# Partners of rotated queries and keys by DMA copies instead of matmuls, the minima ahead of a low half, a take ahead of the sigmoids

## What is computed

```
def _partial_rotary(x, pos):                      # on q (16 heads of 64) and on k (4 heads of 64)
    half = ROT_DIM // 2                           # ROT_DIM = 16
    x1 = x[..., :half];  x2 = x[..., half:ROT_DIM]
    rot = jnp.concatenate([x1 * cos - x2 * sin, x2 * cos + x1 * sin], axis=-1)
    return jnp.concatenate([rot, x[..., ROT_DIM:]], axis=-1)

def _hybrid_layer(h, ...):
    proj = h @ w_in
    (c_val, c_glu, c_gate, q, k, v, a_gate, r_x, r_gate) = jnp.split(proj, split_pts, axis=-1)
    c = c_val * sigmoid(c_glu);  c = silu(layer_norm(causal_depthwise_conv(c)))
    y_conv = (c @ conv_pw_w + conv_pw_b) * silu(c_gate)
    q = _partial_rotary(q, pos);  k = _partial_rotary(k, pos)
    y_attn = sliding_window_sink_attention(q, k, v, sinks) * silu(a_gate)
    y_lru = rg_lru(causal_depthwise_conv(r_x)) * silu(r_gate)       # two sigmoid gates inside
    mixed = jnp.concatenate([y_conv, y_attn, y_lru], axis=-1) @ w_out
    return _layer_norm(ALPHA * h + mixed, ...)
```

## Time and profile before

| | |
|---|---|
| median of 3 runs | 2737.76 us (2734.89 to 2743.21) |
| profiled execution | 2740.33 us, span 2738.5 us, mean granted PE clock 0.997 |
| PE | 2713.5 us busy, 99% |
| DVE, ACT, POOL | 1826.0, 1406.7, 142.8 us busy |
| DMA | 173 GB/s mean |
| second block | about 1941 us to the end; layer 0's projection from 1943, layer 1's from 2345 |

### The profile page before, as it was taken

One profiled execution on the slowest core, in us unless ns is written; L12 is line 12 of the kernel. 1 busy time (PEld: TensorE's weight loads), 2 busy tenths in 40 slices (PEclk: granted clock), 3 DMA queues, 4 the chain that ended last, 5 costly groups with the idle time before them and its releaser, 6 DMA issues.

```text
span 2738.5 us, 45092 instructions
## 1 busy us (share of the span) xinstructions
PE 2713.5 (99%) x16965; PEld 2422.5 (88%) x16965; DVE 1826.0 (67%) x2398; ACT 1406.7 (51%) x2142; POOL 142.8 (5%) x138
## 2 busy tenths in 40 slices
PE   8999999999999999999999999999999999999998
PEld 7888888888888888888888888888999899999897
DVE  7566565655665575665666656755888885789786
ACT  6444444444454454444444444544565774556764
POOL 0000000000000001010010101000000000000000
PEclk9999999999999999999999999999999999999999
DMA  7556655555655556655555655556554445554463
GB/s 232 180 177 184 180 178 178 180 180 177 184 173 187 185 158 181 182 178 180 179 178 179 184 179 179 176 184 187 171 168 128 127 154 172 167 155 146 132 202 129
DMA packets 472600, 474.43 MB, mean 173 GB/s; under 512 B 17674, under 2 KB 467746, under 8 KB 472226
## 3 DMA queue, kind: packets, MB, share of 16 engines
q1 hardware_dynamic: 472244, 472.87, 56.1%
q10 hardware_dynamic: 256, 0.18, 0.0%
HBM read 470.86 MB, written 2.13 MB: 173 GB/s over the span
## 4 chain that ended last, share of the span: by engine, by line
PE 93%; DVE 4%; ACT 2%; issue 1%; DMA 0%; SPq 0%; ACTq 0%; DVEq 0%
PE proj L1280 34%; PE proj L1282 17%; PE proj L1295 9%; PE proj L1467 6%; PE proj L1468 6%; PE proj L1469 6%; PE proj L1297 4%; PE proj L1722 2%; PE ps_s L1371 1%; PE ps_s L1354 1%; PE proj L1724 1%; DVE w_both L2146 1%; PE ps_t L1361 1%; PE ps_s L1372 1%; PE ps_s L1353 1%
## 5 line engine op out<-in xcount | busy, mean ns | idle before, releaser
L1280 PE MATMUL proj<-operand,w_both 128*128 128x512 f32 x4096 | 1453.4, 399 | 2.2 <-DVE w_both L1821 2.1
L1821 DVE TENSOR_TENSOR w_both<-w_raw,w_both 128x1024 fp32r<-128x1024 f32 x644 | 805.6, 1253 | 694.5 <-ACT w_both L673 693.2
L673 ACT ACTIVATE w_both<-w_raw 128x1024 fp32r<-128x1024 f32 x644 | 681.8, 1059 | 920.4 <-PE proj L1282 707.7
L1282 PE MATMUL proj<-operand,w_both 128*128 128x256 f32 x4096 | 1145.9, 280 | 0.0
L1280 PEld LDWEIGHTS proj<-operand,w_both 128*128 128x128 f32 x4096 | 769.0, 188 | 185.0 <-issue 2.4
L1282 PEld LDWEIGHTS proj<-operand,w_both 128*128 128x128 f32 x4096 | 772.9, 189 | 0.8
L1467 PE MATMUL proj<-operand,w_both 128*128 128x272 f32 (+2 forms) x1540 | 450.7, 293 | 0.1
L1468 PE MATMUL proj<-operand,w_both 128*128 128x272 f32 (+2 forms) x1540 | 442.5, 287 | 0.0
L1469 PE MATMUL proj<-operand,w_both 128*128 128x272 f32 (+2 forms) x1540 | 442.2, 287 | 0.0
L2146 DVE TENSOR_TENSOR w_both<-w_raw,w_both 128x1024 fp32r<-128x1024 f32 x226 | 277.5, 1236 | 133.5 <-ACT w_both L883 132.6
L1295 PE MATMUL proj<-w_both,operand 128*128 128x512 f32 x1024 | 363.2, 399 | 0.0
(11 more groups left out here) (383 smaller groups left out, 2055.1 us busy)
## 6 DMA issues: line engine op xcount, KB each, us to landing
w_raw<-in_a_w_in_dram SPq DMA_DIRECT2D x256, 512.0 KB, 3.7
w_raw<-in_w_in_dram SPq DMA_DIRECT2D x160, 512.0 KB, 3.6
w_raw<-in_b_w_in_dram SPq DMA_DIRECT2D x128, 512.0 KB, 3.9
w_raw<-in_kv_w_dram SPq DMA_DIRECT2D x128, 512.0 KB, 4.0
w_raw<-in_a_w_out_dram SPq DMA_DIRECT2D x64, 512.0 KB, 3.5
w_raw<-in_b_w_out_dram SPq DMA_DIRECT2D x64, 512.0 KB, 4.6
w_raw<-in_w_out_dram SPq DMA_DIRECT2D x64, 512.0 KB, 3.5
scratch<-in_a_rel_bias_dram SPq DMA_DIRECT2D x16, 256.0 KB, 3.6
```

The source lines that it names most:

```text
L673: act.activation(w_hi[:, s], w_raw[:, s], ACT.Copy).then_inc(hi_ready, 1)
L1280: pe.matmul(proj[:, 2 * bank + t, :], w_hi[:, s, kk, cols], rhs[:, k, :], start=first and k == 0, stop=False)
L1282: m = pe.matmul(proj[:, 2 * bank + t, 0:S], w_lo[:, s, kk, cols], rhs[:, k, 0:S], start=False, stop=last and end)
L1821: dve.tensor_tensor(w_lo[:, s], w_raw[:, s], w_hi[:, s].bitcast(F32), ALU.subtract).then_inc(pieces_split, 1)
```

## The change

- `perm` and `spread` go, with their two loads. `spread_keys` and `exchange_queries` go from PE: eight f32 matmuls for the keys and eight for the queries in each layer.
- ACT gets `fetch_partners(n, tile)`: four SBUF to SBUF copies of eight partitions each (the two rotated half-ranges of both heads, 2176 B a partition), issued on ACT's own queue: once for the keys behind `shift_kv(0)` and once for each query unit behind its take. The partners go to `rc`, which POOL sets to zero once a layer (`memset`, `pads_ready`); it is used as two buffers, so the third copy on waits for a rotation (`q_rotated`).
- The keys are now rotated once where they stand, by the same `rotate` as the queries (DVE, three instructions of 544 columns for all four heads), and then spread to both halves by four copies of 64 partitions (`spread_keys` on ACT), which `score` and ACT's first `set_sinks` wait for.
- `score(i)` waits for the rotation of its own queries only (`5 * l + i // 2 + 2`), and for all value copies.
- From the second pair on, `score_maxima(i)` stands ahead of the pair's first low half.
- At i = 6 the take of unit 16 stands ahead of the sigmoids instead of two high halves behind the first.

```diff
@@ gpsimd
+            pool.wait_ge(glu_fixed, 1)
+            pool.memset(rc, 0.0).then_inc(pads_ready, 1)
             for l in range(DEPTH):
...
+                if l + 1 < DEPTH:
+                    pool.wait_ge(gate_used, 5 * l + 5)
+                    pool.memset(rc, 0.0).then_inc(pads_ready, 1)
@@ scalar
+                def fetch_partners(n, tile):
+                    half = ROT // 2
+                    for first in (0, HD):
+                        for to, of in ((first, first + half), (first + half, first)):
+                            act.dma_start(partners[n % 2][to:to + half], tile[of:of + half]).then_inc(partners_landed[n % 2], 16)
+
+                def spread_keys():
+                    act.wait_ge(q_rotated, 5 * l + 1)
+                    for h in range(2):
+                        for e in range(2):
+                            act.dma_start(k_spread[HD * h:HD * h + HD, e::2, :], k_raw[HD * e:HD * e + HD])\
+                               .then_inc(k_spread_landed, 16)
+
                 shift_kv(0, k_raw)
+                act.wait_ge(kv_ready, 2 * l + 1)
+                act.wait_ge(pads_ready, l + 2)
+                fetch_partners(0, k_raw)
                 hi(1)
                 affine(3)
                 take_raw(5)
...
-                take(U_Q, att[:, 0:2, :], cols=live)
+                def take_queries(j):
+                    take(U_Q + j, att[:, 2 * j:2 * j + 2, :], cols=live)
+                    act.wait_ge(proj_free, o0 + U_Q + j + 3)
+                    if j == 1:
+                        act.wait_ge(q_rotated, 5 * l + 1)
+                    if j >= 2:
+                        act.wait_ge(q_rotated, 5 * l + j)
+                    fetch_partners(j + 1, att[:, 2 * j:2 * j + 2, :])
+
+                take_queries(0)
                 hi(1)
                 shift_kv(1, v_raw)
-                hi(3)
-                take(U_Q + 1, att[:, 2:4, :], cols=live)
+                hi(2)
+                spread_keys()
+                hi(1)
+                take_queries(1)
                 for j in range(2, 4):
                     hi(4)
-                    take(U_Q + j, att[:, 2 * j:2 * j + 2, :], cols=live)
+                    take_queries(j)
...
                     if i == 6:
                         take_recurrent(3)
                         hi(1)
+                        act.wait_ge(gate_used, 5 * l + 1)
+                        take(unit, a_gates[:, 4:6, :], 0.5, cols=live)
                         act.wait_ge(lru_taken, 4 * l + 4)
                         act.activation(lru_r, lru_r, ACT.Sigmoid)
                         act.activation(lru_i, lru_i, ACT.Sigmoid).then_inc(lru_gates, 1)
@@ tensor
                 for chunk in range(PIECES):
                     pe.wait_ge(in_split, 4 * l + chunk + 1)
                     pieces(U_Q, norm, (chunk,))
-                    if chunk == 1:
-                        spread_keys(0)
-                pieces(U_Q + 1, norm, (0, 1))
-                spread_keys(1)
-                pieces(U_Q + 1, norm, (2, 3))
+                pieces(U_Q + 1, norm, (0, 1, 2, 3))
...
-                pieces(U_Q + 2, norm, (2,))
-                exchange_queries(0, ps_s)
-                pieces(U_Q + 2, norm, (3,))
-                pieces(U_Q + 3, norm, (0,))
-                exchange_queries(1, ps_t)
-                pieces(U_Q + 3, norm, (1, 2))
-                exchange_queries(2, ps_s)
-                pieces(U_Q + 3, norm, (3,))
+                pieces(U_Q + 2, norm, (2, 3))
+                pieces(U_Q + 3, norm, (0, 1, 2, 3))
 
                 def score(i):
-                    pe.wait_ge(q_rotated, 4 * l + (3 if i == 0 else 4))
-                    pe.wait_ge(k_spread_ready, KV_HEADS * l + KV_HEADS)
+                    pe.wait_ge(q_rotated, 5 * l + i // 2 + 2)
+                    pe.wait_ge(k_spread_landed, 16 * 4 * (l + 1))
+                    pe.wait_ge(v_all_ready, 3 * l + 3)
@@ vector
+                def rotate(n, tile, scale, cols):
+                    part = partners[n % 2][:, :, cols]
+                    dve.wait_ge(partners_landed[n % 2], 16 * 4 * ((3, 2)[n % 2] * l + n // 2 + 1))
+                    dve.scalar_tensor_tensor(tile, tile, scale, over(cos[:, cols], 2), ALU.mult, ALU.mult)
+                    step(dve.scalar_tensor_tensor(part, part, scale, over(sin[:, cols], 2), ALU.mult, ALU.mult))
+                    dve.tensor_tensor(tile, tile, part, ALU.add).then_inc(q_rotated, 1)
...
-                rotate_keys(0)
                 lo(1)
                 dve.wait_ge(proj_free, o0 + U_V + 3)
                 fix(v_raw, U_V, kv_fixed)
                 lo(2)
-                rotate_keys(1)
+                rotate(0, k_raw, 1.0, slice(0, T))
...
                 for i in range(PAIRS_2):
-                    lo(1)
                     if i == 0:
-                        rotate_queries(3, ps_t)
+                        lo(1)
+                        rotate_queries(3)
                     score_maxima(i)
+                    if i >= 1:
+                        lo(1)
```

More of the change, by code:

```diff
@@ L118, in shape_constants @@
     cos, sin = np.ones((P, T), np.float32), np.zeros((P, T), np.float32)
-    partner = np.zeros(HD, int)
     for d in range(ROT):
-        partner[d] = d + half if d < half else d - half
         for e in range(2):
@@ L267, in build_program @@
         cos, sin = two.take(T), two.take(T)
-        perm = two.take(P)
-        spread = two.take(4, P)
         twice, head_of = two.take(4 * META), two.take(2)
@@ L421, in build_program @@
         conv_in = sem("conv_in")
-        kv_turned = sem("kv_turned")
-        k_spread_ready = sem("k_spread_ready")
+        partners_landed = [sem(f"partners_landed_{n}") for n in range(2)]
+        k_spread_landed = sem("k_spread_landed")
         v_turned = sem("v_turned")
@@ L565, in _ @@
                 sp.dma_start(sinks[:, l, :], io["attn_sinks_2"][l:l + 1, :].to_broadcast([P, HEADS_2])).then_inc(rows_landed, 16)
[L566 to L567 removed]
+            for dst, name in ((mask_2, "mask_2"), (cos, "cos"), (sin, "sin"), (twice, "twice"), (head_of, "head_of")):
                 at, n = const_at[name]
@@ L1532, in _ @@
                 if l == 0:
-                    pe.wait_ge(consts_2_in, 16 * 7)
-                def spread_keys(r):
-                    pe.wait_ge(kv_ready, 2 * l + 1)
-                    if r == 1:
-                        pe.wait_ge(k_spread_ready, KV_HEADS * l + 2)
-                    for e, banks in ((0, ps_s), (1, ps_t)):
-                        for turned_side in range(2):
-                            m = pe.matmul(banks[:, turned_side, 0:T], spread[:, 2 * e + turned_side, :], k_raw[:, r, :],
-                                          start=True, stop=True)
-                        m.then_inc(kv_turned, 1)
+                    pe.wait_ge(consts_2_in, 16 * 5)
                 def turn_values():
-                    pe.wait_ge(k_spread_ready, KV_HEADS * l + 4)
                     pe.wait_ge(kv_ready, 2 * l + 2)
@@ L1559, in double_meta_values @@
                       .then_inc(v_meta_doubled, 1)
-                def exchange_queries(r, banks):
-                    pe.wait_ge(proj_free, o0 + U_Q + r + 3)
-                    if r == 0:
-                        pe.wait_ge(v_all_ready, 3 * l + 3)
-                    if r >= 2:
-                        pe.wait_ge(q_rotated, 4 * l + r - 1)
-                    for e in range(2):
-                        m = pe.matmul(banks[:, e, live], perm, att[:, 2 * r + e, live], start=True, stop=True)
-                    m.then_inc(q_turned, 1)
                 for chunk in range(PIECES):
```

53 lines of the change are left out of this document (9 added, 44 removed).

## The result

The changed kernel takes 2748.82 us (median of 6 runs, 2746.28 to 2751.29) against 2737.38 us for the kernel before (6 runs, 2734.89 to 2743.21). The ratio is 1.004, 95% interval 1.003 to 1.005: slower by 0.4%, where I had forecast 2731.4, a gain of 6.4 us (0.23%; the prediction rounds it to 0.24), within 2722 to 2738. The measured time is outside the range and on the other side.

What follows compares the result with a forecast made beforehand. PE, busy 99% of the span, was taken as the bound. 23.0 saved - (1.8 + 2.0) - (2.6 + 1.4) - (2.0 + 3.4) - 3.4 = 6.4 us gained, from 2737.76 to 2731.4 us; range 2722 to 2738.

Steps and rivals of the forecast that it cites:

- Matmuls that go: Key and query matmuls removed from PE in both layers: 7.4 + 7.1, together 14.5 us saved.
- The take: Take moved ahead of the sigmoids: PE's stall at the conv sums goes, 5.2 us, plus clock, together 8.5 us.
- What is given back behind it: Conv branch behind the earlier take: later waits of PE return 2.0 us in layer 0, 3.4 in layer 1.
- The price of an issue: Each partner copy's issue on ACT was taken at 0.42 us, four at 1.7 us.
- 1.8 + 2.0: New PE stalls for the first query unit's fourth-piece operand, behind the keys' issues: 1.8 us layer 0, 2.0 layer 1.
- Most places hide it, since ACT waits for PE between its high halves there. One does not: ACT's copy issues cost nothing except at the keys' fetch, where some 1.2 of 1.7 us push the rest back.
- The first transposes: First pair of heads: DVE cannot follow PE, new PE stalls of 2.6 us in layer 0 and 1.4 in layer 1.
- Clock: PE's clock lowered after two of the new stalls, charged as two losses, 3.4 us.
- The issues starve PE: Rival, chance 0.06: keys' fetch between shift_kv and in_hi_of(3) delays PE; slower from 1.0 us an issue, 2750 at 2.56.

Runs made afterwards that it cites:

- the minima alone: Kernel before with only the mask minus scores and minima ahead of the first low half from the second pair on, no copies, take unmoved: 2733.95 us, ratio 0.9994.

## Why the prediction was wrong, step by step

**Matmuls that go: right.** 14.5 us forecast, 14.3 in the shifts.

**The take: right at its place,** 8.5 forecast and 8.4 measured, wait and clock together. What is given back behind it, forecast at 2.0 + 3.4, was 1.3 + 2.6: right in kind, 1.5 us too high. With the minima alone I costed nothing before the sigmoids, and the stretch to there did not change.

**The price of an issue: mis-sized.** I took 0.42 us, "since it is ACT's own". The row was of the right engine and the wrong kind: both of its issues read DRAM. The copies cost 0.63, and 1.25 the first. This turned 1.8 + 2.0 into 3.2 + 3.1 at the operand. At the DRAM price the same formula came out within 0.3 us. I had even asked what the price hangs on, and looked at the size (rightly: it hardly matters) and not at the source. The Trainium skill (DMA: Bandwidth & Descriptors, Anatomy of one DMA) puts the sequencer's dispatch at about 50 ns. Its breakdown is of a DMA issued from GpSimd and lists the making of descriptors beside the dispatch, so I was wrong to hold it against a whole issue on ACT: no issue of the copies is near it, the cheapest being 0.28 us on ACT and 0.52 on POOL, and the traces do not tell the parts of an issue apart.

**"Most places hide it, since ACT waits for PE between its high halves there. One does not": the step that failed.** That sentence disposed of 40 of the 48 issues without a lead worked out for any. One of the places it covers, `spread_keys` and the fetch behind the second unit's take, costs 12.0 us with the clock, more than the whole result. Two things hid it from me. ACT does idle 2 to 3 us between high halves there, but that idle time ends when PE has finished a piece; what is issued only then, behind a take or a long wait, makes the next high half later by its full length. And `spread_keys` adds a wait, for DVE's rotation, with a high half queued behind it on ACT: I followed the removed `exchange_queries` and its waits on PE, and asked of the new wait only whether the copies would land in time. DVE's copy of the turned values had a lead of 0.9 us over PE before (L2285 ended at 2046.09, PE came at 2046.96), while PE was to come 1.9 us earlier; one subtraction of the kind I did for the operand would have shown it.

**The first transposes: right, 2.6 and 1.4 forecast, 2.2 and 1.4 measured,** though by partly false working. The waits stayed at 2.2 and 1.4 in every kernel with copies and the taps in their place, whatever was lost ahead. Kernel after, ACT and DVE:

```profile
2054.08 1.06 ACT L871 ACTIVATE w_both<-w_raw 128x1024 fp32r<-128x1024 f32 x1 [6.17 <-PE proj L1486]
...
2055.17 1.22 DVE L2130 TENSOR_TENSOR w_both<-w_raw,w_both 128x1024 fp32r<-128x1024 f32 x1 [2.40 <-ACT w_both L871]
```

From this low half to the end of the first maxima (2082.2) DVE has no gap, and the high half ahead of it waited for PE: so this wait is DVE's backlog against PE's own way from that release, and it doesn't matter how late PE came to it. The kernel with two taps moved shows it by making it vanish.

**Clock: mis-sized.** Two losses forecast, 3.4 us; there were five, some 11 us. The two short ones, at the doubled values and the first transposes of layer 0, cost 1.6 and 1.7, the price that I took from the kernel before; the three long ones cost more, 2.7 at the operand of layer 0. The losses come with the waits, so an error in a wait of this size is nearly doubled: that is how two wrong terms, of 2.5 and 8.1 us, with 7.6 us of clock beside them, made the 17 us between the forecast and the stretch (18.2, less the 1.5 that I gave back too much in the conv branch).

**The rivals.** "The issues starve PE" was the right mechanism, with 0.06. I worked out that it decides from 1.0 us an issue; it decided at 0.63, because I let it act in one place only.

## What to carry to other kernels

A DMA issue is an instruction of its engine, in order, though no busy time shows it; price it by an issue with the same kind of source, and work out the lead at every place where one is inserted, not only at the tightest one you know. If an engine beside is idle, put issues and the waits ahead of them there: a wait on ACT holds up every high half behind it. Then price each wait of PE of 2 us and more with the lowered clock that may follow.

## What the runs showed of the hardware

- An issue of an SBUF to SBUF copy took ACT 0.63 us (0.58 at four partitions, 0.64 at 64, 1.25 the first of all), POOL 0.52 us (0.59 to 0.64 at 64 partitions); from DRAM it took ACT 0.28 to 0.54. The source is not all of it: SP's issue of 2.56 us read DRAM too, and what made it long stayed open. The copies landed 1.8 to 4.5 us after POOL's issues, 2.6 to 3.1 after the spreads from ACT.
- PE's clock after a wait, in the stretch, over all ten kernels and the one before: all 13 waits of 3.0 us and more were followed by a lowered clock (0.50 to 0.78 over the next 2.6 us); none of those of 1.6 us and less; of the ten from 1.8 to 2.2 us five. The wait of 2.2 us at the first transposes of layer 0 was the same in six kernels and lowered the clock in two of them, so that its length alone does not settle it. What else does stayed open.
